# Partial rotary embedding in the mixer: the partner rows by a DMA and a table with signs, in place of two matmuls with a permutation matrix

## The reference, cut to what matters

```python
def apply_partial_rope(x, cos, sin):
    xf = x.astype(jnp.float32)
    half = ROT_DIM // 2                      # 8
    x1, x2 = xf[..., :half], xf[..., half:ROT_DIM]
    c, s = cos[None, :, None, :], sin[None, :, None, :]
    out = jnp.concatenate([x1 * c - x2 * s, x2 * c + x1 * s, xf[..., ROT_DIM:]], axis=-1)
    return out.astype(x.dtype)
```

## Time and profile before

| | |
|---|---|
| median of 3 runs | 1841.96 us (1841.44 to 1842.23) |
| profiled execution, its own time | 1841.76 us |
| span of that execution, first to last instruction | 1839.9 us |
| mean granted TensorE clock | 0.998 |
| PE busy | 1823.6 us (99%), 11335 instructions |
| DVE busy | 1395.1 us (76%), 1912 |
| ACT busy | 929.8 us (51%), 1274 |
| POOL busy | 81.5 us (4%), 109 |

### The profile page before, as it was taken

The page is one execution under the profiler, slowest core; times in us unless marked ns, Lnnn a source line. Parts: engine busy times, 40 slices in busy tenths (PEclk is TensorE's granted clock), DMA queues, the critical chain, the costliest instruction groups (busy, mean ns, idle before and its releaser), DMA issues.

```text
span 1839.9 us, 28202 instructions
## 1 busy us (share of the span) xinstructions
PE 1823.6 (99%) x11335; PEld 1632.7 (89%) x11341; DVE 1395.1 (76%) x1912; ACT 929.8 (51%) x1274; POOL 81.5 (4%) x109
## 2 busy tenths in 40 slices
PE   9999999999999999999999999999999999999997
PEld 7998998888889988988998899988888888888886
DVE  8875887888778878866888987776767776666566
ACT  6652664435355536643663555455547644444445
POOL 0000000020001000000000000000000000000000
PEclk9999999999999999999999999999999999999999
DMA  6744763462407535743753688732232222221223
GB/s 215 180 125 131 200 165 112 175 152 73 118 24 208 156 106 148 197 148 106 196 140 108 186 217 252 235 125 93 91 138 71 69 92 72 89 88 71 91 69 92
DMA packets 60594, 244.78 MB, mean 133 GB/s; under 512 B 6864, under 2 KB 9456, under 8 KB 49856
## 3 DMA queue, kind: packets, MB, share of 16 engines
q1 hardware_dynamic: 46016, 199.25, 32.3%
q0 software_dynamic: 14032, 43.38, 12.4%
q10 hardware_dynamic: 432, 0.56, 0.1%
HBM read 223.76 MB, written 13.11 MB: 129 GB/s over the span
## 4 chain that ended last, share of the span: by engine, by line
PE 93%; DVE 3%; ACT 1%; issue 1%; DMA 0%; DVEq 0%; ACTq 0%; POOL 0%
PE acc L2580 17%; PE acc L2582 17%; PE acc L2581 17%; PE acc L2588 9%; PE acc L2586 9%; PE acc L2587 9%; PE att L2581 2%; PE att L2582 2%; PE att L2580 2%; PE att L2588 1%; PE att L2586 1%; PE att L2587 1%; PE acc L2855 1%; PE acc L2830 1%; DVE w_lo L1457 0%
## 5 line engine op out<-in xcount | busy, mean ns | idle before, releaser
L1457 DVE TENSOR_TENSOR w_lo<-raw,w_hi 128x2048 fp32r<-128x2048 f32 (+1 forms) x106 | 238.9, 2254 | 56.8 <-ACT w_hi L740 56.5
L740 ACT ACTIVATE w_hi<-raw 128x2048 fp32r<-128x2048 f32 (+1 forms) x106 | 199.3, 1880 | 74.8 <-PE acc L2582 61.0
L2580 PE MATMUL acc<-x_hi,w_hi 128*128 128x512 f32 x488 | 193.1, 396 | 1.5 <-DVE x_lo L1520 1.2
L2582 PE MATMUL acc<-x_hi,w_lo 128*128 128x512 f32 x488 | 190.2, 390 | 0.0
L2581 PE MATMUL acc<-x_lo,w_hi 128*128 128x512 f32 x488 | 190.1, 390 | 0.0
L2586 PE MATMUL acc<-xt_hi,w_hi 128*128 128x256 f32 x684 | 189.1, 276 | 0.0
L2588 PE MATMUL acc<-xt_hi,w_lo 128*128 128x256 f32 x684 | 189.1, 276 | 0.0
L2587 PE MATMUL acc<-xt_lo,w_hi 128*128 128x256 f32 x684 | 189.0, 276 | 0.0
L839 ACT ACTIVATE tmp<-acc 128x256 f32<-128x256 f32 x228 | 86.9, 381 | 120.1 <-PE acc L2588 114.9
L2581 PE MATMUL acc<-g_lo,w_hi 128*128 128x512 f32 x352 | 137.0, 389 | 0.0
L2580 PE MATMUL acc<-g_hi,w_hi 128*128 128x512 f32 x352 | 137.0, 389 | 0.0
(11 more groups left out here) (512 smaller groups left out, 5123.6 us busy)
## 6 DMA issues: line engine op xcount, KB each, us to landing
raw<-in_ffn_down SPq DMA_DIRECT2D x32, 704.0 KB, 4.1
raw_c<-in_ffn_seven SPq DMA_DIRECT2D x37, 512.0 KB, 5.3
raw<-in_ffn_seven SPq DMA_DIRECT2D x33, 512.0 KB, 4.4
raw<-in_ffn_seven POOLq DMA_DIRECT2D x33, 512.0 KB, 7.4
raw<-in_ffn_seven SPq DMA_DIRECT2D x37, 256.0 KB, 4.4
raw<-in_ret_values SPq DMA_DIRECT2D x8, 1024.0 KB, 4.8
raw<-in_ret_out SPq DMA_DIRECT2D x8, 1024.0 KB, 6.6
raw<-in_sb_v SPq DMA_DIRECT2D x8, 1024.0 KB, 4.8
```

The source lines that it names most:

```text
L740: nc.scalar.activation(w_hi[:, slot, at:at + cols], raw[:, slot, 0:cols], ACT.Copy).then_inc(w_hi_ready, 1)
L1457: tt(w_lo[:, slot, at:at + cols], raw[:, slot, 0:cols], w_hi[:, slot, at:at + cols].bitcast(F32), ALU.subtract).then_inc(w_ready, 1)
L2580: mm(dst, still[0], move[0], start=first, stop=False)
L2582: return mm(dst, still[1], move[0], start=False, stop=last)
```

## The change

The permutation matmuls go, with `rot_r`, `stage_hi`, `stage_lo`, `rope_low` and `rotate`. ACT copies the bank once, in float32, to `rope_in` in SBUF, and this copy frees the bank. DVE's cosine product reads `rope_in`. ACT then issues four DMAs for each tile, each of 8 partitions x 2 KB, that move the two exchanged row groups of the two heads from `rope_in` to `rope_turned`; before them it waits for its own copy and for POOL's clearing of `rope_turned`. The sine product reads `rope_turned`, when its four DMAs have landed; the sign is now in the sine table. Both buffers lie where `stage` lies, which attention writes in between, so POOL clears `rope_turned` once before each pass. There are 12 tiles, so 24 matmuls of 512 columns and 12 subtractions on DVE go, and 48 DMAs and 2 memsets come.

```diff
+            pool.wait_ge(seg_done, FFN_SEGS[0])
+            nc.gpsimd.memset(rope_turned[:], 0.0).then_inc(turned_clear, 1)
...
+            pool.wait_ge(mixed, UNITS)
+            nc.gpsimd.memset(rope_turned[:], 0.0).then_inc(turned_clear, 1)
...
             def rope_split(o, side=False):
-                src = att[:, b.k % BANKS, :] if side else acc[:, u.k % BANKS, :]
-                split_acc(stage_hi[:, o * TOK:(o + 1) * TOK], src, 1)
+                src, freed, bank = (att, att_free, b) if side else (acc, acc_free, u)
+                act.wait_ge(seg_done, s.at(1))
+                nc.scalar.activation(rope_in[:, o, :], src[:, bank.k % BANKS, :], ACT.Copy).then_inc(freed, 1)
                 s.next()
-                (b if side else u).next()
+                bank.next()
+
+            def rope_turn(o, half, side=False):
+                if side:
+                    act.wait_ge(att_free, b.at(BANKS))
+                else:
+                    act.wait_ge(acc_free, u.at(BANKS))
+                act.wait_ge(turned_clear, half + 1)
+                for first in range(0, P, HEAD):
+                    for j in range(2):
+                        to, src = (slice(first + ROT * i, first + ROT * (i + 1)) for i in (j, 1 - j))
+                        act.dma_start(rope_turned[to, o, :], rope_in[src, o, :]).then_inc(turned_landed[o], 16)
...
                         rope_split(o, last and (g, o) == (0, 0))
+                        rope_turn(o, int(last), last and (g, o) == (0, 0))
                         if o == 1 and g < N_GROUPS - 1:
                             prep()
...
-            def rope_low(o, side=False):
-                cols = slice(o * TOK, (o + 1) * TOK)
-                src = att[:, b.k % BANKS, :] if side else acc[:, u.k % BANKS, :]
+            def rope_cos(o, side=False):
                 settle()
-                low(stage_lo[:, cols], src, stage_hi[:, cols])
-
-            def rope_cos(o, side=False):
-                src = att[:, b.k % BANKS, :] if side else acc[:, u.k % BANKS, :]
-                tt(t(o), src, rope_a[:, 0, :], ALU.mult).then_inc(att_free if side else acc_free, 1)
                 s.next()
-                (b if side else u).next()
+                if side:
+                    dve.wait_ge(att_free, b.next() + BANKS)
+                else:
+                    dve.wait_ge(acc_free, u.next() + BANKS)
+                tt(t(o), rope_in[:, o, :], rope_a[:, 0, :], ALU.mult)
...
-                dve.wait_ge(att_full, b.next())
-                tt(t(2 + o), att[:, (b.k - 1) % BANKS, :], rope_a[:, 1, :], ALU.mult).then_inc(att_free, 1)
-                dve.wait_ge(att_free, b.at(BANKS))
-                dve.wait_ge(acc_free, u.at(BANKS - split_after))
+                dve.wait_ge(turned_landed[o], 4 * 16 * shifted[o].next())
+                link(tt(t(2 + o), rope_turned[:, o, :], rope_a[:, 1, :], ALU.mult))
                 tt(t(o), t(o), t(2 + o), ALU.add).then_inc(val_ready, 1)
...
-            def rotate(o):
-
-                dst = side_bank()
-                cols = slice(o * TOK, (o + 1) * TOK)
-                mm(dst, rot_r[:], stage_hi[:, cols], start=True, stop=False)
-                mm(dst, rot_r[:], stage_lo[:, cols], start=False, stop=True).then_inc(att_full, 1)
...
-                cos[m], sin[m] = np.cos(ang), np.sin(ang)
+                cos[m], sin[m] = np.cos(ang), np.sin(ang) * f(1 if m % HEAD >= half else -1)
```

More of the change, by code:

```diff
@@ L56 @@
 DIL = 4
+ROT = HEAD // 8
 UNITS = 2 * DIL
@@ L153, in block_kernel @@
         mean_d = sb("mean_d", [P, P])
-        rot_r = sb("rot_r", [P, P], F32R)
         tri_r = sb("tri_r", [P, P], F32R)
@@ L159, in block_kernel @@
         sb("to_line_2", [P, 16])
-        signs = tmp[:, 4 * TOK:4 * TOK + 3 * P].rearrange("p (k c) -> p k c", k=3)
+        signs = tmp[:, 4 * TOK:4 * TOK + 2 * P].rearrange("p (k c) -> p k c", k=2)
         def t(i, width=TOK):
@@ L268, in block_kernel @@
                 va = sb("va", [P, TB, N_GROUPS * GROUP_HEADS, 2, HEAD], F32R, inner)
+                with ExitStack() as under:
+                    rope_in = sb("rope_in", [P, 2, TOK], F32, under)
+                    rope_turned = sb("rope_turned", [P, 2, TOK], F32, under)
                 stage = sb("stage", [P, 4 * KEYS], F32R, inner)
@@ L440, in block_kernel @@
         rest_clear = sem("rest_clear")
+        turned_clear = sem("turned_clear")
+        turned_landed = [sem(f"turned_landed{o}") for o in range(2)]
         h_back = sem("h_back")
@@ L959, in rope_split @@
             def rope_split(o, side=False):
-                src = att[:, b.k % BANKS, :] if side else acc[:, u.k % BANKS, :]
-                split_acc(stage_hi[:, o * TOK:(o + 1) * TOK], src, 1)
+                src, freed, bank = (att, att_free, b) if side else (acc, acc_free, u)
+                act.wait_ge(seg_done, s.at(1))
+                nc.scalar.activation(rope_in[:, o, :], src[:, bank.k % BANKS, :], ACT.Copy).then_inc(freed, 1)
                 s.next()
-                (b if side else u).next()
+                bank.next()
[9 more added lines that the diff above has]
+                        act.dma_start(rope_turned[to, o, :], rope_in[src, o, :]).then_inc(turned_landed[o], 16)
             def rope_done(g, o):
-                b.next()
                 act.wait_ge(val_ready, val.next())
@@ L1838, in qk @@
                             rope_done(g, 0, 0)
-                        if last or (g, o) != (0, 0):
-                            rope_low(o, last and (g, o) == (0, 0))
                         rope_cos(o, last and (g, o) == (0, 0))
@@ L2765, in qk @@
                     for o in range(2):
-                        if last and (g, o) == (N_GROUPS - 1, 1):
-                            dst = bank()
-                            for c in range(DC):
-                                if c == DC // 2:
-                                    pe.wait_ge(op_ready, op.at())
-                                    rotate(0)
-                                    op.next(2)
-                                done = passes(dst, w(DC + c), (x_hi[:, c, :], x_lo[:, c, :]), c == 0, c == DC - 1)
-                            done.then_inc(seg_done, 1)
-                            continue
                         if g or last and o:
                             project(w, o * DC, x)
-                        if (g, o) != (0, 0):
-                            pe.wait_ge(op_ready, op.at(0 if g else 1))
-                            rotate(1 - o)
-                            op.next(2)
                         elif last:
                             gather(units_done, 1)
-            def rotate_last(behind=0):
-                pe.wait_ge(op_ready, op.at(behind))
-                rotate(1)
-                op.next(2)
+                op.next(2 * N_GROUPS)
             def gather(done, filled):
@@ L2908, in _ @@
             qk(True, ahead[0])
-            values(x, plain, {(0, DC - 1): lambda: rotate_last(1), (1, DC - 1): lambda: first_score(1),
+            values(x, plain, {(1, DC - 1): lambda: first_score(1),
                               (2, DC - 1): lambda: scores(1, 1)})
@@ L3357, in constants @@
     c["diag_neg"] = np.where(i >= j, f(NEG), f(0))
-    half = HEAD // 8
-    rot = np.zeros((P, P), f)
-    for m in range(P):
-        d = m % HEAD
-        if d < half:
-            rot[m + half, m] = -1
-        elif d < 2 * half:
-            rot[m - half, m] = 1
+    half = ROT
     c["fold"] = np.hstack([np.zeros((P, HEAD), f), np.vstack([np.eye(HEAD, dtype=f)] * 2), np.zeros((P, HEAD), f)])
-    c["signs"] = np.stack([rot, (i >= j).astype(f), np.ones((P, P), f)], 1)
+    c["signs"] = np.stack([(i >= j).astype(f), np.ones((P, P), f)], 1)
     pos = np.arange(TOK, dtype=f)
```

11 lines of the change are left out of this document (4 added, 7 removed).

## The result

The changed kernel takes 1861.12 us (median of 5 runs, 1860.61 to 1863.45) against 1841.76 (5 runs, 1841.19 to 1842.23): a ratio of 1.0107, with an interval of 1.0095 to 1.0118. It is slower by 1.1%, as forecast in sign, and outside the range of the prediction, which ended at 1852.3.

The account below looks back on a forecast made before the run. PE, busy 99% of the span, bounds the kernel, but where ACT and DVE's loop ends decides. 1841.76 + 1.4 (first pass) + 2.9 (second) + 2.2 (clock) = 1848.3, with 0.2 to the median 1848.5 us; range 1839.5 to 1852.3.

Parts of the forecast that it names:

- Sign, place and chain: Both passes: slower, as ACT's issues delay weight split and rounding, then DVE and PE; loss 1.4 us first, 2.9 second.
- PE's saving: Twelve rotations on PE: 5.8 us of matmuls, with waits at most 7.8 us, if nothing else ends late.
- The price of an issue: ACT's queue: 0.37 us per DMA issue, four make 1.48, and 1.54 per tile with ACT's wait on its copy.
- The loop's steps: ACT and DVE, rounding to rounding: without weight split 5.39 us becomes 4.8, later 4.1 becomes 3.5; with one 7.59 becomes 9.15.
- the path in the first pass: First pass: DVE's split ends at 406.9, PE arrives by 403.7 and waits 3.2 us before the values; loss 1.4 us.
- The landing: Moved rows usable 2.0 us after issue, between 1.7 and 2.4; the second pass's last tile waits for it.
- The clock: Before attention 1's scores PE stands still 7.9 us, its clock halves, and 4.3 us at half speed cost 2.2 us.
- Dearer: Rival: issues of 0.50 and landings of 2.4 us behind slab loads, so 1852.5 us; chance 0.1.
- All of PE's saving arrives: Rival: DVE and ACT keep up at every hand-over, so 1834 us, or by half 1838; chance 0.07.
- The edit does not do what it says: Rival: ACT's wait on its own copy or the memset holds it idle before its issues; price within the range.
- Cheap issues: Rival: issues on ACT's queue cost 0.06 us each, 0.3 per tile, so 1839.5 to 1842 us; chance 0.15.
- The rule on issues: Skill's rule that initiating a DMA is usually small beside it; forecast: a fifth of the landing, four not small.

Follow-up runs that it names:

- the shapes' experiment: Changed kernel with one DMA per tile instead of four, of 8, 16, 32, 64, 72 and 128 partitions in turn, wrong rows moved: 1844.35 us against 1842.54, one run.
- the pairs with and without fillers: Unread matmuls added in PE's wait before attention 1's scores: 16 in the changed kernel without moves, 1840.45 to 1837.81 us; 54 in the changed kernel, 1861.12 to 1861.49.

## Why the prediction was right in kind and wrong in size

- **Sign, place and chain: right.** PE's saving does not arrive; ACT's queue carries the delay by the weight split and the rounding to DVE and PE; the losses sit ahead of the scores of either attention; the sine product of the last tile starts with the landing; the clock stands at 0.50 behind the wait. All of this is in the rows above, and the experiments without moves, with two, with the split ahead of the issues and with the issues on POOL show that it is the cause.
- **The price of an issue: the step that failed.** I took 0.37 us from SP's row and 0.50 as the upper end, with the remark that 8 partitions might be cheaper. It is 0.63, so 2.6 us per tile and not 1.48. That is most of why the first pass costs 6.5 us and not 1.4, and the second 10.3 and not 2.9. The range was closed upwards by rows of another shape, of a transfer from HBM; the shapes' experiment shows that 8 partitions are dearer than 128 (0.69 against 0.52), and that even 128 cost 0.52 on this queue. I had bounded the unseen shape downwards with care, and not upwards.
- **The loop's steps, from one rounding to the next.** Without a split: 370.47 to 375.27, 4.80 us, forecast 4.8. With one: 375.27 to 385.52, 10.25, forecast 9.15; the 1.1 are the dearer issues. First rounding: +5.1 instead of +1.75, since two groups of issues stand ahead of it (3.2 and 2.6 instead of 1.5 each) and the pass began 0.5 late. Two later steps without a split: 4.41 and 3.96 (385.52, 389.93, 393.89 us), forecast 3.5, because now copy, issues and rounding on ACT fill them. The misses, 3.4 + 1.1 + 1.5, are the 6.0 us by which the split of 389.01 came later than forecast (+7.42 against +1.4). With them the path in the first pass was another one: PE was to wait once, 3.2 us ahead of the values, and waits there 1.4, after 3.7 and 3.4 us at the two slabs before.
- **The landing: mis-sized too.** 2.0 us from the last issue's start, bounded by 1.7 and 2.4; measured 3.5. In the second pass the roundings are 2.9, 2.3 and 5.0 us later, counted from the 7.0 at its start, where 1.6, 1.0 and 2.6 were forecast. Then each of the last two tiles takes copy, issues and landing in series: 499.14, 507.83, 515.95 us, 8.7 and 8.1 where I had 6.3 and 5.9. Of each miss of 2.2 to 2.4 us some 1.5 are the landing, the rest is the issues. The wait of PE was 13.8 us and not 7.9. So of the 12.5 us by which the two passes cost more than forecast, the landings make about 3, worked out from these steps, and the issues most of the rest.
- **The clock: right in size.** Forecast 2.2 us, measured 2.4 in the changed kernel; the pairs with and without fillers show 2.0 and 2.4. The assumption that it takes about as long to come back as to go was near: PE ran at half speed from 517.4 to about 522.3 us (0.78 in the stretch from 521 makes 1.3 us at 0.50). That a wait of 3.2 us could not bring it down was wrong: in the changed kernel it stood at 0.50 from 400 to 402 us, behind the wait of 3.4, and in another one behind a wait of 2.1. Nor was it to be 3.2 by my own rows: before, PE went on at 405.47 without a gap, so with 2.9 us less to do it comes there by 402.6 and not 403.7, and waits 4.3 us until 406.9, as long as the idle time behind which I saw the clock fall. Such a fall belonged in the sum or among the rivals; in the changed kernel a later wait hid it.
- **The rivals.** "Dearer" named the right mechanism and stopped at 1852.5, for want of a wider end. "All of PE's saving arrives" is out: even with no moves and the clock kept up the kernel takes 1837.8, near the 1838 given for half the saving. "The edit does not do what it says" is out too: ACT issues within 0.1 us of its copy's end (357.62 + 0.60, 358.24), so neither its wait on the copy nor the memset held it. "Cheap issues" fell with the first row of the queue.
- **The rule on issues.** The measured issue of 0.63 us and the landing of 3.5 stand as about one to six; four issues make 2.6 us beside it. The Trainium skill ("DMA: Bandwidth & Descriptors", section "Issuing engines are not separate DMA queues") calls the initiating time usually small beside the DMA. For four small moves per tile this case disagrees: the step from two moves to four, almost issues alone, costs 10.8 us.

## What to carry to other kernels

Moving work off the busiest engine pays only if what replaces it is not queued ahead of work for which that engine waits: count each DMA issue as an instruction of its queue, by a row with the same number of partitions and the same queue, and where there is none, leave the upper end open (here the issue took 0.63 us where the nearest row, on another queue, had 0.33). Put issues behind the long instruction that others need, since they run beside it. And a saving that ends in a longer wait of TensorE may be taken back by its clock: here a lead of 3.9 us at the scores became 1.1 at the table load behind attention 1.

## What the runs showed of the hardware

- A move between partitions issued on ACT's queue: 0.63 us per issue for 8 partitions (four in a row; 0.69 alone), 0.52 to 0.56 for 16, 32, 64 and 128, 0.83 for 72. Three of the 48 took over 1.2. Usable 3.5 us after the start of the last of four, 3.2 of two.
- Issues that stand behind a running ACTIVATE, and don't wait for it, run beside it (361.30 and 361.43 us above).
- A float32 matmul of 512 columns between others: 0.46 us for itself and 0.41 more for the first of the other type behind it.
- TensorE's clock stood at 0.50 behind waits of 2.1, 3.4, 4.4 and 13.8 us, and at 1.00 behind others of 2.1 and 3.7 (the latter in the changed kernel, until 384.21): the length of a wait alone does not tell. Matmuls without use in the wait kept it at 1.00 in all three trials.
